# Interleaving the modulation of the first norm with its first projection, k-tile by k-tile

## The reference, cut to what matters

```
m = silu(cond) @ mod_w[0] + mod_b[0]          # 3072 values: shift, scale, gate; once for c, once for c_ctx
sh, sc, g = split(m, 3)
h = rms_norm(x, norm_g[0]) * (1 + sc) + sh    # rms_norm: x * rsqrt(mean(x*x) + eps) * norm_g
q, k, v, ... = split(h @ w_in)
```

## Time and profile before

| | |
|---|---|
| median of 3 executions | 3020.62 us (3018.68 to 3025.82) |
| the profiled execution's own time | 3025.83 us |
| its span, first to last instruction | 3024.0 us |
| PE busy, share of the span | 96% |
| DVE, ACT, POOL | 52%, 26%, 23% |
| share of the chain that ended last on PE | 84% |
| first q0 matmul starts | 48.93 us |
| ACT starts to read q0's result | 66.39 us |

### The profile page before, as it was taken

How to read it: one execution, slowest core, us unless ns; L and a number is a source line. 1 busy time by engine, 2 the same in 40 slices (tenths; PEclk the granted TensorE clock), 3 DMA queues, 4 the chain that set the end, 5 groups by cost and what they waited for, 6 DMA issues and landing times.

```text
span 3024.0 us, 27502 instructions
## 1 busy us (share of the span) xinstructions
PE 2903.3 (96%) x11064; PEld 1469.6 (49%) x11064; DVE 1567.7 (52%) x1967; ACT 777.7 (26%) x970; POOL 688.9 (23%) x458
## 2 busy tenths in 40 slices
PE   6998999988899999998999999999999999999998
PEld 3563445644455444445764455454444444444443
DVE  4657885537756776735764522257343333343003
ACT  4116772124401201124631132132112222220001
POOL 0003774013500222225241100111102222222110
PEclk9999999999999999999999999999999999999999
DMA  6001001210042211113121011002211111112111
GB/s 235 28 21 49 1 1 29 63 37 1 1 176 103 102 38 42 42 49 95 33 95 49 29 61 59 34 15 97 98 42 42 42 42 42 42 41 109 49 38 56
DMA packets 43501, 168.42 MB, mean 56 GB/s; under 512 B 5648, under 2 KB 6160, under 8 KB 39152
## 3 DMA queue, kind: packets, MB, share of 16 engines
q1 hardware_dynamic: 38160, 151.57, 14.6%
q0 software_dynamic: 5216, 15.11, 1.8%
HBM read 149.88 MB, written 19.40 MB: 56 GB/s over the span
## 4 chain that ended last, share of the span: by engine, by line
PE 84%; DVE 10%; ACT 2%; issue 2%; DMA 1%; SPq 0%; POOL 0%; DVEq 0%; ACTq 0%
PE ps L1010 36%; PE ps L1003 11%; PE ps L1865 9%; PE ps L1691 3%; PE ps L1651 2%; PE ps L1537 2%; PE ps L1353 2%; PE ps L1391 2%; PE ps L1258 2%; PE ps L1126 1%; PE ps L1274 1%; PE ps L1289 1%; DVE arena L2646 1%; PE ps L1682 1%; DVE x_ctx L2646 1%
## 5 line engine op out<-in xcount | busy, mean ns | idle before, releaser
L1010 PE MATMUL ps<-arena 128*128 128x512 f32 x1160 | 509.3, 593 | 3.2 <-DVE arena L2858 1.6
L1010 PEld LDWEIGHTS ps<-arena 128*128 128x128 f32 x1160 | 219.8, 190 | 278.8 <-issue 274.4
L1003 PE MATMUL ps<-arena 128*128 128x512 f32 x896 | 332.9, 532 | 4.2 <-ACT arena L1966 2.0
L1010 PE MATMUL ps<-x_lat,arena 128*128 128x512 f32 x720 | 318.4, 592 | 0.4 <-DVE arena L2548 0.4
L1003 PEld LDWEIGHTS ps<-arena 128*128 128x128 f32 x896 | 169.2, 190 | 165.3 <-issue 156.7
L1010 PEld LDWEIGHTS ps<-x_lat,arena 128*128 128x128 f32 x720 | 136.7, 190 | 173.0 <-issue 171.7
L1010 PE MATMUL ps<-x_lat,x_ctx 128*128 128x512 f32 x432 | 190.5, 593 | 2.8 <-ACT arena L2023 2.8
L1865 PE MATMUL ps<-arena 128*128 128x512 f32 x416 | 179.8, 592 | 0.0
L2832 DVE SCALAR_TENSOR_TENSOR x_ctx<-arena,vectors,x_ctx 128x1024 f32<-128x1024 f32 x120 | 169.7, 1414 | 3.5
L1353 PE MATMUL ps<-arena 64*128 64x512 f32 x504 | 150.4, 677 | 21.9 <-DVE x_ctx L2646 9.7
L1949 ACT ACTIVATE arena<-x_lat 128x1024 f32<-128x1024 f32 x40 | 41.8, 1049 | 435.7 <-PE ps L1865 224.9
(11 more groups left out here) (358 smaller groups left out, 4445.6 us busy)
## 6 DMA issues: line engine op xcount, KB each, us to landing
arena<-in_wall SPq DMA_DIRECT2D x188, 512.0 KB, 4.4
residual_store<-x_lat SPq DMA_DIRECT2D x12, 1024.0 KB, 7.3
x_lat<-residual_store SPq DMA_DIRECT2D x12, 1024.0 KB, 6.9
x_lat<-in_xl_in SPq DMA_DIRECT2D x8, 1024.0 KB, 10.2
arena<-in_wdown SPq DMA_DIRECT2D x12, 512.0 KB, 4.6
x_lat<-expanded_bias POOLq DMA_DIRECT2D x32, 128.0 KB, 2.9
arena<-expanded_bias POOLq DMA_DIRECT2D x32, 128.0 KB, 3.3
out<-x_lat SPq DMA_DIRECT2D x8, 512.0 KB, 3.0
```

Source lines behind the costliest of these rows:

```text
L1003: mm = pe.matmul(ps[:, o + c:o + c + n], W[:, ring_of(g) % WSLOTS, k, :], rhs(k, c, n), start=(k == 0), stop=(k == KT - 1))
L1010: mm = pe.matmul(ps[:, bank * BANK:(bank + 1) * BANK], weights[:, k, :], tokens[:, k, :], start=(start and k == 0), stop=(k == 3), skip_gr ...
```

## The change

The residual and the context are loaded first. Then come the modulation tiles in pairs (shift tile k and scale tile 8 + k), each pair on a semaphore of its own, with the weights of `q0` behind the first pair. The norm uses `token_sums` and `over_partitions` as `n1` does, with 8 `keep_warm` ahead of it; the row sums of pairs 0 and 1 stand between its sums and its spreading. ACT copies the spread reciprocals to SBUF. The small columns, the shift and scale of a k-tile (`first_modulation(k)`), its application (`modulate_tile`) and its share of the projection now go k by k (`first_projection`). Two PSUM areas for rows and two for columns alternate.

The core of the diff:

```
# SP
+ for k in range(0, KT, 2): load XL[k:k+2]; load XCv[k:k+2]
+ for k in range(KT):
+     for m in (k, KT + k): load mod_weights(m) -> mod_in[k]
+     if k == 0: load_weight(MOD0)
+ ... if g == MOD0 + 4: sp.wait_ge(rope_in, 32); load ROPE

# PE
+ if ph == "n0": pe.wait_ge(sq_used, 4)
+ keep_warm(4 * BANK, {"n0": 8, ...}[ph])
+ def mod_rows(k):
+     pe.wait_ge(mod_in[k], 32)
+     if k >= 2: pe.wait_ge(rows_in_sbuf, k - 1)
+     for x, m in enumerate((k, KT + k)):
+         for kk in range(KT): pe.matmul(ps[r, ROWS_PS[k % 2] + ...], SC32[:, kk, :], weights[:, kk, :], ...)
+         mm.then_inc(w_mod, 1)
+ def mod_columns(k):
+     pe.wait_ge(rows_in_sbuf, k + 1)
+     if k >= 2: pe.wait_ge(mod_ready, k - 1)
+     two matmuls of MROWS[k % 2] with ROW_SUM -> COLS_PS[k % 2]; mm.then_inc(mod_cols, 1)
+ norm_sums("n0", lambda: [mod_rows(k) for k in range(2)])
+ def first_projection():
+     mod_columns(0)
+     for k in range(KT):
+         if k + 2 < KT: mod_rows(k + 2)
+         if k + 1 < KT: mod_columns(k + 1)
+         pe.wait_ge(h_ready, k + 1)
+         for x in range(3 * k, 3 * k + 3): mm = product_part(("evA", "qk", 0), ..., PARTS[x])

# ACT
+ rows_to_sbuf(0)
+ root("n0", 0, RT[:, 0:TOK // P])
+ rows_to_sbuf(1)
+ act.wait_ge(rs_wide, RS_STEP["n0"])
+ act.activation(NRS("n0"), ps[:, o:o + TOK], ACT.Copy)
+ for k in range(KT):
+     if k + 2 < KT: rows_to_sbuf(k + 2)      # waits for w_mod, 2 * (k + 2) + 2
+     act.wait_ge(mod_ready, k + 1)
+     modulate_tile(0, 0, k)

# DVE
- first_norm(): mean_square over 128x1280, multiply by x for each k, all of the modulation after k = 0
+ first_norm(): token_reciprocals("n0"), wait for ACT's copy, then for each k:
+     H[k] = XCv[k] * rs, XL[k] * rs; first_modulation(k)
```

More of the change, by code:

```diff
@@ L318, in program @@
         w_mod = sem("mod_weights_used")
[L319 to L322, removed]
+        late_in = [sem(f"mod_weights{m}_{m + 8}_and_late_weights_in") for m in range(3)]
+        down_in = [sem(f"mod_weights{m}_{m + 8}_and_down_weights_{x}_in")
+                   for m, x in ((3, "a11_a12"), (4, "a21_a22"), (5, "rest"))]
+        rope_in = sem("mod_weights6_14_and_rope_in")
+        bmask_in = sem("mod_weights7_15_and_band_mask_in")
+        mod_in = late_in + down_in + [rope_in, bmask_in]
+        mod_cols = sem("modulation_columns_summed")
         late_t = sem("late_mod_rows_summed")
@@ L1048, in over_partitions, with norm_sums @@
                 return mm
-            def norm_sums(ph):
+            def norm_sums(ph, between=lambda: None):
                 t, o = tile(ph, "nrm")
@@ L1060, in norm_sums @@
                 mm.then_inc(ps_ready, 1)
+                between()
                 pe.wait_ge(rs_small, RS_STEP[ph])
@@ L1078, in _ @@
             pe.wait_ge(silu_c, 2)
[L1079 to L1101, removed]
@@ L1102, in _ @@
-            row_sums(MOD0 // 4 - 1).then_inc(ps_ready, 1)
-            keep_warm(3 * BANK, 3)
+            def mod_rows(k):
+                pe.wait_ge(mod_in[k], 32)
+                if k >= 2:
+                    pe.wait_ge(rows_in_sbuf, k - 1)
+                for x, m in enumerate((k, KT + k)):
+                    weights = mod_weights(m)
+                    for kk in range(KT):
+                        r = slice(32 * (kk % 4), 32 * (kk % 4) + 32)
+                        mm = pe.matmul(ps[r, ROWS_PS[k % 2] + x * P:ROWS_PS[k % 2] + (x + 1) * P], SC32[:, kk, :], weights[:, kk, :],
+                                       start=(kk < 4 and x == 0), stop=(kk >= 4), skip_group_check=True)
+                    mm.then_inc(w_mod, 1)
@@ new lines, in mod_columns @@
+            def mod_columns(k):
+                pe.wait_ge(rows_in_sbuf, k + 1)
+                if k >= 2:
+                    pe.wait_ge(mod_ready, k - 1)
+                for x in range(2):
+                    mm = pe.matmul(ps[:, COLS_PS[k % 2] + 2 * x:COLS_PS[k % 2] + 2 * x + 2], MROWS[k % 2][:, x * P:(x + 1) * P], ROW_SUM,
+                                   start=True, stop=True)
+                    if x == 0 and k == KT - 1:
+                        mm.then_inc(ps_ready, 1)
+                mm.then_inc(mod_cols, 1)
@@ L1127, in product_part @@
                                  start=(k == 0), stop=(k == KT - 1), skip_group_check=True)
+            def first_projection():
+                mod_columns(0)
+                for k in range(KT):
+                    if k + 2 < KT:
+                        mod_rows(k + 2)
+                    if k + 1 < KT:
+                        mod_columns(k + 1)
+                    pe.wait_ge(h_ready, k + 1)
+                    for x in range(3 * k, 3 * k + 3):
+                        mm = product_part(("evA", "qk", 0), even_weight("evA", "q0"), hrow, x, PARTS[x])
+                mm.then_inc(ps_ready, 1)
             def gate_pair(ph, j, t_next, between):
@@ L1178, in even_half @@
                 for m, name in enumerate(("q0", "q1", "q2", "q3", "k")):
-                    if first or m:
-                        product((ph, "qk", m), even_weight(ph, name), hrow, full,
-                                (lambda k: (h_ready, k + 1)) if first and m == 0 else None)
+                    if first and m == 0:
+                        first_projection()
+                    elif m:
+                        product((ph, "qk", m), even_weight(ph, name), hrow, full)
                     if first and m >= 1:
@@ L1974, in _, with rows_to_sbuf @@
             squares("n0")
[L1975 to L1981, removed]
+            def rows_to_sbuf(k):
+                act.wait_ge(w_mod, 2 * k + 2)
+                if k >= 2:
+                    act.wait_ge(mod_cols, k - 1)
+                act.activation(MROWS[k % 2], ps[:, ROWS_PS[k % 2]:ROWS_PS[k % 2] + 2 * P], ACT.Copy).then_inc(rows_in_sbuf, 1)
+            rows_to_sbuf(0)
+            root("n0", 0, RT[:, 0:TOK // P])
+            rows_to_sbuf(1)
+            t, o = tile("n0", "nrm")
+            act.wait_ge(rs_wide, RS_STEP["n0"])
+            act.activation(NRS("n0"), ps[:, o:o + TOK], ACT.Copy).then_inc(ps_free[t % 2], 1)
+            for k in range(KT):
+                if k + 2 < KT:
+                    rows_to_sbuf(k + 2)
+                act.wait_ge(mod_ready, k + 1)
+                modulate_tile(0, 0, k)
             def even_half(ph, first):
@@ L2329, in add_squares @@
             def add_squares(ph, k):
-                if k == 0 or (k == KT - 1 and ph != "n0"):
+                if k == 0 or k == KT - 1:
                     return
@@ L2449, in finish_mod, with first_modulation, first_norm @@
                 dve.scalar_tensor_tensor(MA[:, layer], MOD[:, layer, 8:16, :], 1.0, ng, ALU.add, ALU.mult).then_inc(mod_ready, 1)
[L2451 to L2454, removed]
+            def first_modulation(k):
+                both = MOD[:, 0, 0:MOD0, :].rearrange("p (x k) a -> p x k a", x=2)[:, :, k, :]
+                b = vcol("mod_b", 0, MOD0).rearrange("p (x k) -> p x k", x=2)[:, :, k:k + 1].to_broadcast([P, 2, 2])
+                dve.wait_ge(mod_cols, k + 1)
+                link(dve.tensor_tensor(both, ps[:, COLS_PS[k % 2]:COLS_PS[k % 2] + 4].rearrange("p (x a) -> p x a", x=2), b, ALU.add))
+                dve.scalar_tensor_tensor(MA[:, 0, k, :], MOD[:, 0, KT + k, :], 1.0, vcol("norm_g", k).to_broadcast([P, 2]),
+                                         ALU.add, ALU.mult).then_inc(mod_ready, 1)
+            def first_norm():
+                token_reciprocals("n0")
+                t, o = tile("n0", "nrm")
+                rs = NRS("n0")
+                dve.wait_ge(ps_free[t % 2], t // 2 + 1)
+                for k in range(KT):
+                    dve.tensor_tensor(H[:, k, LAT:TOK], XCv[:, k, :], rs[:, LAT:TOK], ALU.mult)
+                    dve.tensor_tensor(H[:, k, 0:LAT], XL[:, k, :], rs[:, 0:LAT], ALU.mult).then_inc(hn, 1)
+                    first_modulation(k)
+                t, _ = tile("mod0", "mod")
+                dve.wait_ge(mod_ready, KT)
                 dve.engine_nop().then_inc(ps_free[t % 2], 1)
+                dve.wait_ge(hn, KT)
             link(dve.memset(SC32, 0.0))
```

93 lines of the change are left out of this document (36 added, 57 removed).

## The result

The changed kernel takes 3036.43 us (median of 6 executions, 3031.81 to 3037.51); the kernel before, run beside it, 3026.84 us (6 executions, 3018.68 to 3032.52). The ratio is 1.0031, with an interval of 1.0017 to 1.0046: slower by 9.6 us, 5.1 to 13.9. The profiled execution has a span of 3035.7 us against 3024.0.

What follows compares the result with a forecast made beforehand. TensorE, busy for 96% of the span, bounds the kernel, so q0's end decides: -7.7 at the start, +17.7 in the loop, 1.7 and 3.4 for low clock, total +15.1; 3020.6 + 15.1 = 3035.7 us, range 3025 to 3045.

Steps and rivals of the forecast that it cites:

- the ring: q0's loop: row sums of k+2, copy, modulation and projection run serially, 5.56 us a round for five rounds; +17.7 us.
- PE's own sum of 3.77: q0's loop: row sums, columns and projection alone, 1.08 + 0.53 + 2.16 us a round, if ACT's work were ahead.
- The front: Opening up to q0: the new transfers and norm start q0 at 41.2, 7.7 us earlier than before.
- 3.8 us at half rate: Idle matmuls ahead of the token sums: PE comes from idleness, so 5.8 records run slowly, then 10.2 at 0.33 us.
- rival (c): Norm's root: a drain behind the table load delays it 1.4 us, total +16.5; 5 in 100.
- The clock: Idle gaps in q0's opening lower the clock: one spell ahead of the first k-tile, 1.7 us, two in the rounds, 3.4.
- rival (b): q0's loop: a spell of low clock in every round, +20.2 us, up to +28; 16 in 100.
- +15.1 forecast: Whole kernel: earlier start, serial rounds and low-clock spells together make it 15.1 us slower.
- the 76 to 82 of the forecast: End of q0: ACT reads it at 76 to 82 us instead of 66.39.
- one of its own signs of being wrong: Behind q0: the prediction is wrong if q0's late end is taken back downstream.
- nothing but the shift would be changed behind q0: After ACT's reading of q0: all later stages stay the same, only moved in time.
- Rival (d): q0's loop: transfers pace it, a pair every 2.6 us, q0 ends at 48.3, -17.9 us; 3 in 100.

Runs made afterwards that it cites:

- Experiment 1: Changed kernel with ScalarE modulating k-tile k before copying the rows of pair k+2, instead of after; 3024.07 us, 0.9989 of the kernel before.
- experiment 2: Changed kernel, order kept, with matmuls whose result nobody reads ahead of TensorE's wait for `h_ready` in rounds 0 to 5; 3029.68 us, 1.0008 of the kernel before.
- experiment 4: Changed kernel without the 8 idle matmuls ahead of the token sums; 3038.66 us, ratio 1.0036 to the kernel before.
- experiment 12: experiment 11 with 4 idle matmuls and pair 0's row sums replacing 8 idle matmuls ahead of the token sums; 3016.27 us, 0.9973 of the kernel before.
- experiment 3: Changed kernel with all row sums and columns ahead of the projection, all row copies ahead of the modulation; 3019.71 us, 0.9971 of the kernel before.
- experiment 11: Changed kernel with ScalarE's order as in Experiment 1 and pair 3's row sums ahead of the first projection; 3018.94 us, 0.9985 of the kernel before.
- the pure delay of 18 us: Kernel before with 33 instead of 3 idle matmuls ahead of q0; 3044.89 us, grown by 0.63%.

## Why the prediction was right

**The direction and the cause.** The forecast was a ring of row sums, copy, modulation and projection that makes each round longer than PE's work. Experiment 1 removes the ring by swapping the two steps of ScalarE's loop and the rounds become 3.8 us, PE's own sum of 3.77; experiment 2 keeps the ring at the full clock and they are 5.54 for a forecast of 5.56. This is shown, not argued.

**The front.** Each step against the trace: last squares' pair from 19.28 (forecast 19.7), idle matmuls from 19.19 (19.5), token sums from 26.07 (26.7) to 30.7 (31.4), q0 at 40.24 (41.2). The one microsecond is made of small pieces; half of it is the idle matmuls (7.04 us for 7.2) and a start 0.3 earlier. The forecast gave those matmuls 3.8 us at half rate without a row that says so; the size fell out about right, but the same eight matmuls took between 7.04 and 8.11 us in the six traces that keep them (the changed kernel's two, experiments 1, 2, 3 and 11). That they lay on the path was right: without them q0 starts 2.7 us earlier (experiment 4), and with the shorter front of experiment 12 it starts 3.5 us earlier. The table load had work due behind it, and the root started 0.02 us after its end, as the trace of before had it and not 1.4 us later as rival (c) had it:

```profile
32.17 1.28 ACT L1964 ACT_TABLE_LOAD   x1
33.47 0.21 ACT L1964 ACTIVATE softmax_stats<-softmax_stats 128x10 f32<-128x10 f32 x1
```

**The clock: the term that was mis-sized.** I counted one spell ahead of the first k-tile and two in the five rounds behind, 1.7 us each, 5.1 in all. In the changed kernel there was one at the first and one in each of the next four; rounds of 7.2 less 5.56 are 1.65 us a spell, as priced, but the first cost 8.52 - 5.56 = 3.0, since the low clock also covered the row sums behind it. Together 9.5 us. Filling the holes took q0's reading from 84.98 to 75.2, 9.8 us and so about this amount. So in the opening rival (b) was nearer than the forecast: five of six groups had their spell, in the second trace too, where the third group was the spared one and not the sixth. The Trainium skill, "TensorE: Matmul & The Clock Gate", section "Loop structure matters more than you think", shows a loop in which a long wait for a transfer ahead of every matmul, 8 us in its example, leaves the engine cold. It does not speak of waits as short as these, 1.6 us for ScalarE; that they sufficed is what the traces here add.

**The size of the whole.** +9.6 us was measured (5.1 to 13.9), +15.1 forecast. In the opening the traces show more, not less: +18.6 in the first pair, against 15.1. ACT's reading of q0 came at 84.98, behind the 76 to 82 of the forecast, and one of its own signs of being wrong came in part: 6.9 of these 18.6 us are not found at the end of the span. The step that failed is that nothing but the shift would be changed behind q0. The base was one trace, with the earliest q0 and the longest rest of four: one in four of these openings loses 7 us, and the rest carries 47.8 to 58.0 us at the low clock, so it moves by 6 us from trace to trace. The forecast hung on that single trace. That 3035.7 lies so near to 3036.43 is in part luck: the kernel before measured 3026.84 and not the 3020.62 from which the forecast started, and the delay that was forecast too small in the opening met a rest that came out shorter.

What stays open is why the changed kernel's rest is shorter. It is shorter by spells of low clock, as the table shows; whether the change brings fewer of them, or its two traces happened to have fewer, two traces do not tell. The early readings of experiments 1, 3, 11 and 12 with still shorter rests, and the pure delay of 18 us that cost 19.1 (11.5 to 26.6) where the changed kernel's similar one cost 9.6 (5.1 to 13.9), speak for the change rather than for the point in time; the overlapping intervals do not prove it. No run changed the transfers or the norm alone.

**The transfers** neither bound nor helped: no row sum in the loop waited for one, as forecast. Rival (d) never came near.

## What to carry to other kernels

When two engines hand work back and forth, write down each one's list for one round and look whether an instruction that only prepares a later round stands ahead of one that the current round needs; here that single order put ScalarE's copy and modulation between two stretches of TensorE's work in every round, 5.54 us for 3.8. Starting dense work earlier is no gain if it then runs in pieces: the time at which it ends counts, and most holes of 1.6 us cost as much again through the clock. Before a forecast of a few microseconds, see more than one trace of the kernel before.

## What the runs showed of the hardware

- Behind holes of 1.16 us the granted clock was at 0.50 (the 1.2 of its two levels 1.2 and 2.4 GHz) in experiments 3, 11 and 12, each time with columns ahead of the hole, matmuls of only 2 columns. A hole of 1.48 us cost nothing in the first trace of the kernel before, nor did one of 2.08 us ahead of q0 in its third trace, where idle matmuls stood ahead of the hole (2.39 us for the first six records, clock 1.00). The changed kernel's hole of 1.58 us at 77.56 cost nothing either, with columns ahead of it. Length alone does not tell which hole costs a spell, and neither do the columns.
- Idle matmuls of 384 columns in the holes held the clock at 1.00 for 37 us, in a stretch where without them five rounds lost 9.5 us (experiment 2 against the changed kernel).
- Behind q0, fourteen traces of ten kernels differ by up to 11.3 us (2946.3 to 2957.6), and all but 3 us of it is the time at the low clock.
- One kernel, the same instructions, and q0 read at 66.4, 67.3, 66.9 and 73.9 us: in the trace with 73.9 the window from 44 to 56 us stands at a granted clock of 0.50, in that with 66.9 at 1.00. The columns at the low clock took 1.87 us for 8 records against 1.05, the row sums 1.08 for 16 against 0.64.
